# Delta rule and gMLP block: prologue between uv's weight chunks, factors and masks in PSUM, gMLP later in the solve, two of four out_e chunks behind the scan's last step

## The chip, the cores and the metric

The kernel runs on one core of one Trainium2 chip. The metric is the device time of one launch in microseconds. The kernel before has a median of 1855.72 us over 3 runs (1851.77, 1855.72 and 1855.77); its profiled execution took 1853.88 us, of which the profile's span covers 1852.1 us.

## The reference, cut to what matters

The program is a whole two-part network for 256 tokens of width 1024: one block with attention and a large expert layer, then two layers of which the first ("even") has a gMLP half and a gated delta rule half. Only this even layer is touched:

```python
proj = hn @ w_in_e[i]
a_uv, b_qkv, b_z, b_beta, b_a = jnp.split(proj, split_at, axis=-1)
a_out = gmlp_spatial_gate(jax.nn.gelu(a_uv), gmlp_v_gain[i], gmlp_ws[i], gmlp_bs[i])
b_out = gated_deltanet(b_qkv, b_z, b_beta, b_a, gdn_conv[i], gdn_a_log[i],
                       gdn_dt_bias[i], gdn_out_gain[i])
h = h + jnp.concatenate([a_out, b_out], axis=-1) @ w_out_e[i]
...
# gmlp_spatial_gate: v is layer-normed in groups, mixed over the tokens of a chunk, gates u
s = jnp.einsum('gts,bnsgc->bntgc', w, v) + b_s.T[None, None, :, :, None]
return u * s.reshape(bsz, seq, A_WIDTH_2)
...
# chunk_gated_delta_rule: 4 heads, 4 chunks of 64 tokens
decay = jnp.where(causal, jnp.exp(jnp.where(causal, diff, 0.0)), 0.0)
a = jnp.where(strict, jnp.einsum('bhnid,bhnjd->bhnij', k_beta, k) * decay, 0.0)
t_mat = a + jnp.eye(c, dtype=f32)
u = solve(t_mat, v_beta)
w = solve(t_mat, k_beta * jnp.exp(gc)[..., None])
qk = jnp.einsum('bhnid,bhnjd->bhnij', q, k) * decay
def step(state, inp):
    v_new = u_c - jnp.einsum('bhck,bhkv->bhcv', w_c, state)
    o_c = (jnp.einsum('bhck,bhkv->bhcv', q_c, state)
           + jnp.einsum('bhij,bhjv->bhiv', qk_c, v_new))
    state = state * gl_c[..., None, None] + jnp.einsum('bhck,bhcv->bhkv', k_c, v_new)
    return state, o_c
```

## The kernel before, in words

All weights stream through a ring of four slots, one "chunk" of 128 rows by up to 1024 columns at a time, in the order of one list (`PLAN`; `FIRST[name]` is where a matrix begins). The SP queue loads a chunk, ACT rounds it to a high part (`w_hi`, L1208), POOL takes the rest (`w_lo`, L1680), and TensorE (PE) multiplies. A chunk with its weights as moving operand is twelve matmuls of 512 columns (L606 to L608). ACT may round into a slot only when PE has used its last content (`used`), and every engine works through its instructions strictly in the written order, so a wait in front of one instruction holds up all behind it on that engine.

The even layer has, in PE's order, these stages: `qkv_e` with a short convolution on VectorE (DVE); `uv`, 8 chunks for the gMLP half, with six fills of transposes that bring q, k and v to token-major form (`token_major`, tiles `Qt`, `Kt`, `Vt`) ahead of chunk 2; then the delta rule's prologue; the solve; the scan; and `out_e`'s 8 chunks.

- The prologue: `gcT` (cumulated log decay, L975), a diagonal `DG` on DVE (L2322), the decay rows `gcrow` (L981), their differences (`D0`, `decA`, `decAT`, L2327 to L2330) and exponents (ACT, L1503, L1505); key lengths `l2_r` (squares on ACT, L1475, a power on POOL, L1825), three scalings on DVE (`k_map`, `q_map`, `kb_map`, L2309), `QDt` and `KBE` on ACT (L1514), and eight groups of transposes (L996) whose results DVE and ACT copy in turn (`fT`). Masks are multiplied in on DVE (L2344). ACT also applies gelu to uv's four banks (`ev_uv`, L1482, L1486) and squares them for the layer norm (L1497); POOL normalizes them (L1759 to L1771, semaphore `gv`).
- The solve is the list `SOLVE` of 21 products, `a`, `aT`, `N2` and so on to `qkT` (L1046), each for two halves of the tokens: eight matmuls, in six PSUM banks in turn. Where a result is in `PLAIN`, ACT evacuates it, else DVE. At `MIX_AT` the gMLP mix (L1026) stands ahead of the product, DVE makes its result (`OC`, L2358) ahead of the next one's, and at `GMLP_T_AT` stand the transposes of that result.
- The scan has four steps (`wS` L1063, `dS` L1073, `o_T` L1077). After the scan, `head_norm` (ACT squares L1544, POOL power L1844, DVE L2407) gives the other half of `OC`, which is transposed (L679) and streamed into `out_e`'s chunks 4 to 7. Chunks 0 to 3 need only the gMLP half:

```python
for c in range(SEQ // G_CH):
    ...
    m.then_inc(sem("o_T"), 1)
    out_chunk(c)
```

## Time and profile before

| what | value |
|---|---|
| median of 3 runs | 1855.72 us |
| profiled execution, its span | 1853.88 us, 1852.1 us |
| PE, DVE, ACT, POOL busy, share of the span | 95%, 51%, 50%, 57% |
| chain that ended last, by engine | PE 86%, DVE 6%, ACT 3%, POOL 2%, issue 2% |
| uv chunks 2 to 7 | 1119.0 to 1135.6 us |
| prologue, PE busy | 1135.6 to 1155.4 us, 10.6 us |
| solve | 1155.4 to 1206.6 us |
| scan with out_e chunks 0 to 3 | 1206.6 to 1233.1 us |
| wait, transposes, out_e chunks 4 to 7 | 1233.1 to 1255.2 us |

Times count from the span's start. The chain is followed backwards from the last instruction, so an engine's share of it says how much of the span hangs on that engine; busy shares alone do not.

### The profile page before, as it was taken

To read this page: it belongs to the slowest core of one execution; us is meant where nothing else is said; L and a number is where in the kernel's file an instruction comes from. 1 tells how busy PE (TensorE), PEld (TensorE's weight loads), DVE (VectorE), ACT (ScalarE), POOL (GpSimd) and SP (SyncE) were. 2 spreads that over 40 slices of the span, in tenths; PEclk is the share of its full clock that TensorE was granted. 3 is DMA by queue.
4 is the path that set the end of the run, shared out by engine and by line. 5 is a ranking of instruction groups with operands and counts; after the bars stand their busy time and mean duration, and the time that the engine had idled before them with its cause. 6 is when DMAs were issued, how large, how long until landed. Compare 5 with 4: busy or idle time off the path is not lost.

```text
span 1852.1 us, 32185 instructions
## 1 busy us (share of the span) xinstructions
...
## 2 busy tenths in 40 slices
...
GB/s 200 175 80 114 117 213 168 184 182 182 147 139 137 143 143 180 193 193 194 193 193 193 172 191 78 8 84 154 184 190 187 164 159 125 36 163 182 190 185 111
DMA packets 81027, 288.23 MB, mean 156 GB/s; under 512 B 9264, under 2 KB 9264, under 8 KB 80432
## 3 DMA queue, kind: packets, MB, share of 16 engines
...
q10 hardware_dynamic: 432, 1.05, 0.1%
...
## 4 chain that ended last, share of the span: by engine, by line
PE 86%; DVE 6%; ACT 3%; POOL 2%; issue 2%; DMA 0%; DVEq 0%; ACTq 0%; POOLq 0%
PE acc L606 14%; PE acc L607 14%; PE acc L608 14%; PE col L642 11%; PE col L643 11%; PE col L644 11%; PE mb L899 3%; POOL w_lo L1680 1%; PE acc L1046 1%; PE col L1046 1%; ACT hT_hi L1232 1%; PE mb L679 1%; ACT w_hi L1208 1%; PE mb L738 1%; PE mb L880 0%
## 5 line engine op out<-in xcount | busy, mean ns | idle before, releaser
L1680 POOL TENSOR_TENSOR w_lo<-w_raw,w_hi 128x1024 fp32r<-128x1024 f32 (+1 forms) x410 | 989.6, 2434 | 372.8 <-ACT w_hi L1208 372.6
L1208 ACT ACTIVATE w_hi<-w_raw 128x1024 fp32r<-128x1024 f32 (+1 forms) x539 | 565.6, 1053 | 407.1 <-PE acc L608 368.0
L642 PE MATMUL col<-hT_hi,w_hi 128*128 128x256 f32 x1632 | 467.7, 287 | 2.3 <-DVE hT_lo L1886 1.8
L644 PE MATMUL col<-hT_hi,w_lo 128*128 128x256 f32 x1632 | 461.6, 283 | 0.0
L643 PE MATMUL col<-hT_lo,w_hi 128*128 128x256 f32 x1632 | 461.5, 283 | 0.0
L642 PEld LDWEIGHTS col<-hT_hi,w_hi 128*128 128x128 f32 x1632 | 312.5, 192 | 5.4 <-issue 2.2
L643 PEld LDWEIGHTS col<-hT_lo,w_hi 128*128 128x128 f32 x1632 | 312.7, 192 | 2.4
L644 PEld LDWEIGHTS col<-hT_hi,w_lo 128*128 128x128 f32 x1632 | 312.3, 191 | 0.0
L606 PE MATMUL acc<-w_hi,W_hi 128*128 128x512 f32 x512 | 199.2, 389 | 0.0
L607 PE MATMUL acc<-w_lo,W_hi 128*128 128x512 f32 x512 | 199.2, 389 | 0.0
L608 PE MATMUL acc<-w_hi,W_lo 128*128 128x512 f32 x512 | 199.2, 389 | 0.0
L606 PE MATMUL acc<-w_hi,hT_hi 128*128 128x512 f32 (+2 forms) x432 | 171.0, 396 | 15.5 <-POOL w_lo L1680 6.0
L1722 POOL TENSOR_SCALAR_AFFINE_SELECT WST<-WST 128x512 f32<-128x512 f32 x1 | 1.7, 1712 | 318.8 <-DMA WST<-in_gmlp_w 318.8
L2453 DVE CAST H_hi<-H_q 128x256 fp32r<-128x256 f32 x64 | 29.9, 467 | 292.4 <-ACT H_q L1561 292.4
L607 PE MATMUL acc<-w_lo,hT_hi 128*128 128x512 f32 (+2 forms) x432 | 168.4, 390 | 0.0
L608 PE MATMUL acc<-w_hi,hT_lo 128*128 128x512 f32 (+2 forms) x432 | 167.6, 389 | 0.0
L2229 DVE TENSOR_TENSOR w_lo<-w_raw,w_hi 128x1024 fp32r<-128x1024 f32 x128 | 156.4, 1222 | 2.1 <-ACT w_hi L1208 1.9
L2207 DVE TENSOR_TENSOR W_lo<-act_e,W_hi 128x256 fp32r<-128x256 f32 x128 | 54.5, 426 | 145.8 <-ACT W_hi L1417 145.2
L606 PEld LDWEIGHTS acc<-w_hi,hT_hi 128*128 128x128 f32 x432 | 83.2, 193 | 37.0 <-issue 14.9
L606 PEld LDWEIGHTS acc<-w_hi,W_hi 128*128 128x128 f32 x512 | 96.1, 188 | 20.1
L607 PEld LDWEIGHTS acc<-w_lo,W_hi 128*128 128x128 f32 x512 | 96.1, 188 | 19.9
L608 PEld LDWEIGHTS acc<-w_hi,W_lo 128*128 128x128 f32 x512 | 96.1, 188 | 19.8
...
## 6 DMA issues: line engine op xcount, KB each, us to landing
w_raw<-in_expert_u SPq DMA_DIRECT2D x128, 512.0 KB, 3.4
w_raw<-in_expert_v SPq DMA_DIRECT2D x128, 512.0 KB, 3.4
w_raw<-in_w_mlp SPq DMA_DIRECT2D x128, 512.0 KB, 3.4
...
```

The costliest lines, as they stand in the source:

```text
L606: mm(o, hi(t), w_hi[:, s, a:b], start=first, stop=False)
L607: mm(o, hi(t), w_lo[:, s, a:b], start=False, stop=False)
L608: m = mm(o, lo(t), w_hi[:, s, a:b], start=False, stop=last)
L642: mm(o, wh[:, k, :], hi[:, k, :], start=k == 0, stop=False)
L643: mm(o, wh[:, k, :], lo[:, k, :], start=False, stop=False)
L644: m = mm(o, wl[:, k, :], hi[:, k, :], start=False, stop=k == KD - 1)
L899: m = mm(mb[s % 2][:, t * P:(t + 1) * P], hot2[:, s % 2, t, :], hot1[:, s % 2, t, :], start=True, stop=True)
L1046: m = mm((acc + col)[n % 6][:, h * P:(h + 1) * P], maps[lhsT][:, t, h, :], maps[rhs][:, t, h, :], start=True, stop=True)
L1208: f(w_hi[:, s, 0:w], w_raw[:, s, 0:w], ACT.Copy).then_inc(sem(f"hi{s}"), 1)
L1680: g.tensor_tensor(w_lo[:, s, 0:w], w_raw[:, s, 0:w], w_hi[:, s, 0:w].bitcast(F32), ALU.subtract).then_inc(sem(f"lo{s}"), 1)
L2207: v.tensor_tensor(lo[:, q, :], act_e[:, c, :], hi[:, q, :].bitcast(F32), ALU.subtract).then_inc(sem("W_lo"), 1)
L2229: v.tensor_tensor(w_lo[:, s, :], w_raw[:, s, :], w_hi[:, s, :].bitcast(F32), ALU.subtract).then_inc(sem(f"lo{s}"), 1)
```

## The change

What it does, engine by engine:

- PE: `gcT` stands between the fourth and fifth fill of `token_major`, in the banks `col`; the decay rows stand ahead of uv's chunk 3 (`decay_rows`), the two halves of the feature maps ahead of chunks 6 and 7 (`feature_maps(0)`, `(1)`). The solve starts after chunk 7 without waiting for all of uv's banks; its bank order is changed, and its second to fifth half products wait for uv's evacuations one by one. The mix goes from the fifth product to the twelfth, the gMLP transposes from the eleventh to the sixteenth. In the scan, chunk 0 stands behind step 0, none behind step 1, chunk 1 behind step 2, chunks 2 and 3 behind step 3.
- DVE: the decay work comes ahead of the scalings. Masks 0, 1 and 3 and the three factors are copied into PSUM (`map_mask`, `map_scale`), and five multiplications read them there; so does `DG`. A tile `decN` (mask 3 times `decATm`) is new, and `N1T` is made from the PSUM product and `decN`.
- ACT: exponents, `QDt`, `KBE` and the odd `fT` copies come ahead of uv's gelus, with the first three `out_e` chunks' `w_hi` between; the layer norm's squares go behind `N2T`, and write to `N8`. The chunks' `w_hi` behind the scan's steps are placed one by one.
- POOL: the key lengths and `VBt` go ahead of uv's chunk 6, the gain on `Z` ahead of `out_e`'s chunk 0, the rest of the delta and gMLP maps ahead of its chunk 3, with `KDt` first. The second half's output norm stands ahead of chunk 6.

```diff
-MIX_AT, GMLP_T_AT = 4, 10
+MIX_AT, GMLP_T_AT = 11, 15
...
+        solve_banks = [col[1]] + acc + [col[0]]
+        map_scale = [col[0][:, 8 * i:8 * i + 8] for i in range(3)]
+        map_mask = [col[0][:, P * (i + 1):P * (i + 2)] for i in range(3)]
...
+                maps = [[(h * P, QKVF[:, 4 * m + h, t * P:(t + 1) * P]) for h in range(G_H)]
+                        for m in range(3) for t in range(NT)]
+                fills("tok", maps[0:4])
+                for t in range(NT):
+                    mm(col[t][:, 0:G_H], masks[:, 2, :], stat[:, 16 + 4 * t:20 + 4 * t], start=True,
+                       stop=True).then_inc(sem("gcT"), 1)
+                fills("tok", maps[4:6], n0=4)
+            def decay_rows():
+                pe.wait_ge(sem("ones"), 1)
+                for t in range(NT):
+                    pe.wait_ge(sem("diag"), t + 1)
+                    mm(col[t][:, :], ones[:, :], DG[:, t, :, :].rearrange("p h f -> p (h f)"),
+                       start=True, stop=True).then_inc(sem("gcrow"), 1)
+            def feature_maps(t):
...
+            row_group("uv", None, before=(2, token_major, 3, decay_rows, 6, lambda: feature_maps(0),
+                                          7, lambda: feature_maps(1)))
...
+                    if 1 <= n <= 4:
+                        pe.wait_ge(sem("ev_uv"), upto("ev_uv", n))
...
-                out_chunk(c)
+                for k in ((0,), (), (1,), (2, 3))[c]:
+                    out_chunk(k)
...
+            split_to(FIRST["uv"] + 7)
+            act.wait_ge(sem("gc"), 2)
+            f(egc[:, :], gc[:, :], ACT.Exp).then_inc(sem("egc"), 1)
+            for t in range(NT):
+                act.wait_ge(sem("gdiff"), 2 * t + 1)
+                f(decA[:, t, :, :], decA[:, t, :, :], ACT.Exp, scale=-1.0).then_inc(sem("dec"), 1)
+                act.wait_ge(sem("gdiff"), 2 * t + 2)
+                f(decAT[:, t, :, :], decAT[:, t, :, :], ACT.Exp).then_inc(sem("dec"), 1)
+                act.wait_ge(sem("glast"), t + 1)
+                f(gl[:, 8 * t:8 * t + 8], gl[:, 8 * t:8 * t + 8], ACT.Exp).then_inc(sem("gl"), 1)
             split_to(FIRST["uv"] + 8)
+            act.wait_ge(sem("egc"), upto("egc", 1))
+            def times_egc(dst, src, ready, name):
+                act.wait_ge(sem(ready), upto(ready, 1))
+                for t in range(NT):
+                    for h in range(G_H):
+                        x = f(dst[:, t, h, :], src[:, t, h, :], ACT.Copy,
+                              scale=egc[:, 4 * t + h:4 * t + h + 1])
+                x.then_inc(sem(name), 1)
+            def odd_maps(ns):
+                for n in ns:
+                    act.wait_ge(sem("fT_T"), upto("fT_T", n + 1))
+                    f(fT[:, n % 4, n // 4, :, :].rearrange("p h d -> p (h d)"), mb[1][:, :],
+                      ACT.Copy).then_inc(sem("fT_A"), 1)
+            times_egc(QDt, Qt, "q_map", "qd")
+            split_to(FIRST["out_e"] + 1)
+            odd_maps((1, 3))
+            times_egc(KBE, KBt, "kb_map", "kbe")
+            odd_maps((5, 7))
+            split_to(FIRST["out_e"] + 3)
...
+                if s == 4:
+                    gate_squares()
+                if result == "N8":
+                    act.wait_ge(sem("v_ss"), upto("v_ss", 1))
...
-                split_to(FIRST["out_e"] + (6 if t == 0 else KD))
+                split_to(FIRST["out_e"] + 5 + t)
...
+            split_to(FIRST["out_e"] + 7)
             stream_hi("oc", range(2, 4))
+            split_to(FIRST["out_e"] + KD)
...
+                if j == FIRST["uv"] + 6:
+                    key_lengths()
+                    beta_values()
...
-                if j == FIRST["out_e"]:
+                    gate_gain()
+                if j == FIRST["out_e"] + 3:
                     delta_and_gmlp_maps()
...
-                if j in (FIRST["out_e"] + 6, FIRST["mlp0"]):
-                    t = int(j == FIRST["mlp0"])
+                if j in (FIRST["out_e"] + 5, FIRST["out_e"] + 6):
...
+                then(v.tensor_copy(gc[:, 4 * t:4 * t + 4], col[t][:, 0:4]), "gc")
                 then(v.tensor_tensor(DG[:, t, :, :], over(ident[:, :], [P, 4, P], 1),
-                                     over(gc[:, 4 * t:4 * t + 4], [P, 4, P], 2), ALU.mult), "diag")
+                                     over(col[t][:, 0:4], [P, 4, P], 2), ALU.mult), "diag")
+            for n in (4, 5):
+                dve.wait_ge(sem("tok_T"), upto("tok_T", n + 1))
+                then(v.tensor_copy(token[n], mb[n % 2][:, :]), "tok_E")
             for t in range(NT):
...
+            for i, m in enumerate((0, 1, 3)):
+                go(v.tensor_copy(map_mask[i], masks[:, m, :]))
+            go(v.tensor_copy(map_scale[2], stat[:, 32:40]))
...
+            go(v.tensor_copy(map_scale[0], sq16[:, 8:16]))
+            then(v.tensor_scalar(map_scale[1], sq16[:, 0:8], G_DK ** -0.5, None, ALU.mult))
+            scale_groups(Kt, Kt, map_scale[0], "k_map")
+            scale_groups(Qt, Qt, map_scale[1], "q_map")
+            scale_groups(KBt, Kt, map_scale[2], "kb_map")
...
+            for n, (dst, src, m) in enumerate(((decA, decA, 0), (decATm, decAT, 1),
+                                               (decN, decATm, 2))):
+                then(v.tensor_tensor(groups(dst), groups(src), over(map_mask[m], [P, 8, P], 1),
                                      ALU.mult))
+                if n == 0:
+                    even_maps((4, 6))
...
-                        then(v.tensor_tensor(four(aT, t), src, four(decATm, t), ALU.mult))
-                        then(v.tensor_tensor(four(N1T, t), four(aT, t),
-                                             over(masks[:, 3, :], [P, 4, P], 1), ALU.mult), "sv_E")
+                        go(v.tensor_tensor(four(aT, t), src, four(decATm, t), ALU.mult))
+                        then(v.tensor_tensor(four(N1T, t), src, four(decN, t), ALU.mult), "sv_E")
```

The prediction speaks of three places. The first is PE around uv's last chunk. Before, the last matmuls of chunk 7 (`L606` to `L608` lines) are followed by the whole prologue and the solve (`L1046`):

```order
L607 MATMUL acc<-w_lo,hT_hi 128x512
L608 MATMUL acc<-w_hi,hT_lo 128x512
L975 MATMUL mb<-stat,masks 128x4 x2
L981 MATMUL acc<-DG,ones 128x512 x2
L996 MATMUL mb<-ident,Kt 128x128 x4
L996 MATMUL mb<-ident,KBt 128x128 x4
L996 MATMUL mb<-ident,Qt 128x128 x4
L996 MATMUL mb<-ident,QDt 128x128 x4
```

After the change, chunk 6's last matmuls (lines L611 to L613 now) are followed by the second half of the feature maps, and chunk 7 begins behind them:

```order
L612 MATMUL acc<-w_lo,hT_hi 128x512
L613 MATMUL acc<-w_hi,hT_lo 128x512
L997 MATMUL mb<-ident,Kt 128x128 x4
L997 MATMUL mb<-ident,KBt 128x128 x4
L997 MATMUL mb<-ident,Qt 128x128 x4
L997 MATMUL mb<-ident,QDt 128x128 x4
L611 MATMUL acc<-w_hi,hT_hi 128x512
L612 MATMUL acc<-w_lo,hT_hi 128x512
```

What moved is the prologue's PE work, from behind chunk 7 to in front of chunks 3, 6 and 7; the copies of `fT` that its groups wait for now hold up uv's chunks.

The second place is ACT between the squares of k and the solve. Before, uv's gelus (`UV`) and their table come first:

```order
L1482 ACT_TABLE_LOAD
L1482 ACTIVATE UV<-acc,sum_91 128x512
L1486 ACTIVATE UV,gsum<-acc,sum_91 128x128 x4
L1482 ACTIVATE UV<-acc,sum_91 128x512
L1486 ACTIVATE UV,gsum<-acc,sum_91 128x128 x4
L1492 ACT_TABLE_LOAD
L1492 ACTIVATE egc<-gc 128x8
L1497 ACTIVATE N2T,gvar<-UV,gsum 128x128 x8
L1503 ACTIVATE decA<-decA 128x512
```

After the change the gelus come last, behind the copies of `fT` and two chunks' `w_hi`:

```order
L1506 ACTIVATE QDt<-Qt,egc 128x128 x8
L1218 ACTIVATE w_hi<-w_raw 128x1024
L1514 ACTIVATE fT<-mb 128x512 x2
L1506 ACTIVATE KBE<-KBt,egc 128x128 x8
L1514 ACTIVATE fT<-mb 128x512 x2
L1218 ACTIVATE w_hi<-w_raw 128x1024 x2
L1526 ACT_TABLE_LOAD
L1526 ACTIVATE UV<-acc,sum_91 128x512
L1530 ACTIVATE UV,gsum<-acc,sum_91 128x128 x4
L1526 ACTIVATE UV<-acc,sum_91 128x512
L1530 ACTIVATE UV,gsum<-acc,sum_91 128x128 x4
L1560 ACTIVATE N_164<-acc 128x512
```

What moved: a whole group of ACT work is now between PE's feature maps and the evacuation of uv's banks, and the squares (`L1497` before) are no longer in it.

The third place is DVE around the twelfth and thirteenth product of the solve (`Y+` and `YT+`). Before, the additions to `YI` and `YIT` and the masked `L1T`, `L2T` follow each other; the gMLP result `OC` stood eight products earlier:

```order
L2393 TENSOR_TENSOR L1T<-aT,masks 128x512
L2397 TENSOR_TENSOR YI<-col,YI 128x512
L2393 TENSOR_TENSOR L2T<-aT,masks 128x512
L2397 TENSOR_TENSOR YIT<-acc,YIT 128x512
L2393 TENSOR_TENSOR L2T<-aT,masks 128x512
L2397 TENSOR_TENSOR YIT<-acc,YIT 128x512
```

After the change `OC` stands between them:

```order
L2443 TENSOR_TENSOR L1T<-aT,masks 128x512
L2447 TENSOR_TENSOR YI<-col,YI 128x512
L2409 SCALAR_TENSOR_TENSOR OC<-mb,cols,UV 128x128 x8
L2443 TENSOR_TENSOR L2T<-aT,masks 128x512
L2447 TENSOR_TENSOR YIT<-col,YIT 128x512
L2443 TENSOR_TENSOR L2T<-aT,masks 128x512
L2447 TENSOR_TENSOR YIT<-acc,YIT 128x512
```

What moved is eight instructions on DVE, into the one run of DVE work that PE waits for late in the solve.

## Rows read from the trace of the kernel before

**Rows 1.** The page, the chain that ended last by engine.

```profile
PE 86%; DVE 6%; ACT 3%; POOL 2%; issue 2%; DMA 0%; DVEq 0%; ACTq 0%; POOLq 0%
```

**Rows 2.** Windows: length, busy of PE, PEld, DVE, ACT, POOL, PE clock, DMA.

```profile
1119.00:1135.60 16.60, 16.54 (x74) 13.36 (x72) 3.86 (x6) 9.66 (x42) 10.64 (x6) 1.00 0.45 148
1135.60:1155.40 19.80, 10.60 (x41) 6.94 (x41) 10.81 (x20) 13.85 (x48) 10.27 (x14) 0.74 0.01 1
1155.40:1168.00 12.60, 7.54 (x49) 7.35 (x50) 12.33 (x10) 2.75 (x9) 8.23 (x3) 0.73 0.00 0
1168.00:1205.50 37.50, 35.64 (x313) 35.00 (x311) 19.57 (x35) 14.69 (x23) 6.31 (x3) 1.00 0.07 17
...
1242.00:1255.20 13.20, 13.08 (x48) 10.56 (x49) 2.58 (x5) 4.40 (x7) 6.11 (x3) 0.83 0.16 44
```

**Rows 3.** Timeline of DVE: start, length, instruction, idle before and its releaser.

```profile
1132.59 0.17 DVE L2314 TENSOR_SCALAR sq<-sq 128x8 f32<-128x8 f32 x1 [12.60 <-POOL sq L1825]
...
1138.46 2.01 DVE L2322 TENSOR_TENSOR DG<-ident,gc 128x512 f32<-128x512 f32 x1
...
1145.27 0.43 DVE L2329 TENSOR_SCALAR decA<-D 128x512 f32<-128x512 f32 x1
...
1156.33 2.80 DVE L2344 TENSOR_TENSOR decATm<-decAT,masks 128x1024 f32<-128x1024 f32 x1
...
1174.27 2.16 DVE L2358 SCALAR_TENSOR_TENSOR OC<-mb,cols,UV 128x128 f32<-128x128 f32 x8
```

**Rows 4.** Groups, 1113 to 1168 us: busy us, mean ns, idle before.

```profile
L1680 POOL TENSOR_TENSOR w_lo<-w_raw,w_hi 128x1024 fp32r<-128x1024 f32 x5 | 11.8, 2388 | 4.6 <-ACT w_hi L1208 4.6
...
L1208 ACT ACTIVATE w_hi<-w_raw 128x1024 fp32r<-128x1024 f32 x5 | 5.0, 1050 | 0.5 <-PE acc L608 0.5
...
L2387 DVE TENSOR_TENSOR N1T<-aT,masks 128x512 f32<-128x512 f32 x2 | 3.5, 1768 | 0.1
...
L1497 ACT ACTIVATE N2T<-UV,gsum 128x128 f32<-128x128 f32 x8 | 3.1, 387 | 0.0
...
L1825 POOL TENSOR_TENSOR sq<-sq,minus_half 128x16 f32<-128x16 f32 x1 | 2.9, 2927 | 0.1
...
L1514 ACT ACTIVATE QDt<-Qt,egc 128x128 f32<-128x128 f32 x8 | 2.4, 386 | 0.0
...
L2309 DVE TENSOR_TENSOR KBt<-Kt,stat 128x1024 f32<-128x1024 f32 x1 | 1.2, 1224 | 0.0
```

**Rows 5.** Timeline of POOL in the prologue, with idle before and its releaser.

```profile
1144.44 1.75 POOL L1761 TENSOR_TENSOR gvar<-gvar,minus_half 128x8 f32<-128x8 f32 x1
...
1149.85 2.35 POOL L1771 TENSOR_TENSOR UV<-UV,rows 128x1024 f32<-128x1024 f32 x1
1155.12 2.94 POOL L1776 TENSOR_TENSOR KDt<-Kt,kdf 128x1024 f32<-128x1024 f32 x1 [2.91 <-DVE kdf L2341]
```

**Rows 6.** Timeline of ACT: first gelu of uv, table load behind the last.

```profile
1133.54 0.69 ACT L1482 ACTIVATE UV<-acc,sum 128x512 f32<-128x512 f32 x1 [6.42 <-PE acc L608]
...
1137.72 1.28 ACT L1492 ACT_TABLE_LOAD   x1
```

**Rows 7.** Timeline of PE in the solve and at the scan's start.

```profile
1164.24 3.78 PE L1046 MATMUL col<-N,N1T 128*128 128x128 f32 x16 [5.06 <-DVE N1T L2387]
...
1169.70 1.95 PE L1026 MATMUL mb<-UV,WST 128*128 128x128 f32 x16
...
1191.91 2.05 PE L1046 MATMUL col<-P,YIT 128*128 128x128 f32 x16 [1.40 <-DVE YIT L2397]
...
1206.61 1.13 PE L1073 MATMUL mb<-Vn,KDt 64*128 64x128 f32 x8 [1.42 <-DVE Vn L2424]
```

**Rows 8.** Windows of the scan: chunk 0, step 2, end of chunk 3 to chunk 4.

```profile
1208.68:1213.20 4.52, 4.52 (x13) 3.32 (x12) 0.68 (x1) 0.00 (x0) 0.00 (x0) 0.62 0.49 169
...
1220.20:1224.20 4.00, 4.00 (x33) 3.53 (x32) 1.42 (x4) 2.22 (x9) 2.58 (x2) 1.00 0.02 4
...
1233.10:1242.10 9.00, 2.06 (x9) 1.57 (x8) 1.83 (x5) 3.39 (x11) 3.61 (x3) 0.68 0.25 83
```

More of the change, by code:

```diff
@@ L1470, in _ @@
             act.wait_ge(sem("tok_E"), upto("tok_E", 4))
-            for m, (src, squares) in enumerate(((Qt, D0), (Kt, N2))):
+            for m, src in enumerate((Qt, Kt)):
                 for t in range(NT):
@@ L1500, in _ @@
-            x.then_inc(sem("v_ss"), 1)
-            for t in range(NT):
-                act.wait_ge(sem("gdiff"), 2 * t + 1)
-                f(decA[:, t, :, :], decA[:, t, :, :], ACT.Exp, scale=-1.0).then_inc(sem("dec"), 1)
-                act.wait_ge(sem("gdiff"), 2 * t + 2)
-                f(decAT[:, t, :, :], decAT[:, t, :, :], ACT.Exp).then_inc(sem("dec"), 1)
-                act.wait_ge(sem("glast"), t + 1)
-                f(gl[:, 8 * t:8 * t + 8], gl[:, 8 * t:8 * t + 8], ACT.Exp).then_inc(sem("gl"), 1)
@@ L1523, in _, with gate_squares @@
-            times_egc(KBE, KBt, "kb_map", "kbe")
+            def gate_squares():
+                act.wait_ge(sem("v_mean"), upto("v_mean", 1))
+                for t in range(NT):
+                    for g in range(M_G):
+                        x = f(N8[:, t, g, :], UV[:, t, 512 + g * P:512 + (g + 1) * P], ACT.Square,
+                              bias=gsum[:, 4 * t + g:4 * t + g + 1],
+                              accum_out=gvar[:, 4 * t + g:4 * t + g + 1])
+                x.then_inc(sem("v_ss"), 1)
+                split_to(FIRST["out_e"] + 4)
@@ L1773, in delta_and_gmlp_maps @@
                                 ALU.mult).then_inc(sem("gv"), 1)
-                pool.wait_ge(sem("kd_factor"), upto("kd_factor", 1))
-                g.tensor_tensor(heads(KDt), heads(Kt), per_head(kdf[:, :]), ALU.mult).then_inc(
-                    sem("kd"), 1)
                 pool.wait_ge(sem("dec"), 4)
@@ L2299, in _ @@
                                  over(stat[:, 60:64], [P, NT, 4], 1), ALU.mult), "g_ready")
-            copies("tok", [m[:, t, :, :].rearrange("p h d -> p (h d)") for m in (Qt, Kt, Vt)
-                           for t in range(NT)])
+            token = [m[:, t, :, :].rearrange("p h d -> p (h d)") for m in (Qt, Kt, Vt)
+                     for t in range(NT)]
+            copies("tok", token[0:4])
             dve.wait_ge(sem("masks"), 20)
```

122 lines of the change are left out of this document (44 added, 78 removed).

## The prediction, made before the changed kernel was run

> **What bounds the kernel now.** I read the page's chain of waits first: 86% of the span hangs on TensorE (PE) [rows 1]. So the change is worth what it takes out of PE's order, and the stages around it are read window by window [rows 2]. In uv's six last chunks PE is full (16.54 of 16.60 us, clock 1.00), while VectorE (DVE) works 3.86 us. Then comes the prologue, 19.80 us with PE busy 10.60 at a mean granted clock of 0.74. In the next 12.60 us it is busy 7.54 at 0.73. From 1168.0 the solve keeps it full (35.64 of 37.50 us). The timeline tells what PE waits for: 5.06 us for N1T before the third product at 1164.24, then 3.78 us for that product at half clock, and 1.40 us for YIT at 1191.91 [rows 7]. In the scan one window stands out: 9.00 us from chunk 3's end to chunk 4, PE busy 2.06 [rows 8].
>
> The groups say why DVE is slow: N1T takes 1768 ns in the mean [rows 4], but one of its two took 0.69; DG took 2.01 and decATm 2.80 [rows 3], for work that takes 0.69 and 1.22 elsewhere (KBt, same shape: 1224 ns [rows 4]). Each slow one ran while POOL worked on SBUF: decATm from 1156.33 to 1159.13, KDt on POOL to 1158.06 [rows 3, 5]; the rest, 1.07 us, is about its own length.
>
> **The change, part by part**, in times of the trace before.
>
> 1. *uv ends later.* Before, chunk 7 ends at 1135.4. Now the prologue's PE work stands before it: 10.60 us at 0.74 is 7.8 us at most at full clock [rows 2]; half of the decay rows' and transposes' time was at the low clock, which gives about 6.1. To it come the waits that PE now has in uv, for the copies of fT. The scalings wait for the key lengths, which came at 1132.5 [rows 3] and lose two w_lo of 2.39 in front of them: 1127.7 or sooner. DVE comes from the decay rows (chunk 2 ends at 1119.1 + 2.8 = 1121.9, the first row takes 0.9): two rounds of 0.7, twice 0.43 and 0.17 (3.6 us with their gaps), then mask and factor copies, some 1.5 by their columns: 1128.1. Three maps of 1.22 [rows 4] end at 1131.9, when chunk 5 ends. QDt on ACT (2.4 us) waits for the second map and ends at 1133.0; a w_hi of 1.05 stands behind it [rows 4], and a copy of fT of some 0.6. So PE waits 0.8 + 0.3 us for ACT and 0.3 us at the third group for DVE. 6.1 + 1.4 = 7.5: uv ends at 1142.9. (Bounds: 6.1, no wait; 7.8 + 1.4 + 2.4 for a w_lo on POOL in front of DVE's small copies of kdf, 11.6.)
> 2. *uv's evacuation.* ACT makes the last fT copy, two w_hi (2.1) and a table load (1.28 [rows 6]) and reaches the first gelu at 1144.2. From first gelu to last took 1133.54 to 1137.7, 4.15 us, half of it for two banks [rows 6]. So banks are free at 1144.9, 1146.3, 1146.9 and 1148.4. The product aT waits for the second, takes 0.9 per half (35.64 us in 313 matmuls of 16 per product, 1.8 [rows 2]), then DVE makes aT and N1T from PSUM, 0.7 each: the third product starts at 1148.7 instead of 1164.24 [rows 7]. **Gain 15.5.**
> 3. *Third and fourth product*, to the next stage: before 1164.24 to 1169.70, 5.46, with 3.78 for the first [rows 7]. Now PE's idle pieces are under 1.2 us each, so I take the full clock: 1.8 + 1.8, 0.4 of waiting for the second N1T and 0.35 for YI, YIT (DVE, two of 1.22, the first behind KDt on POOL). 4.35. **Gain 1.1** (bounds 0 and 1.8).
> 4. *Rest of the solve.* Before 1169.70 to 1206.61, 36.9 us, mix and transposes in it [rows 7]; both are moved, not removed. DVE now makes OC (2.16 [rows 3]) between the additions of the twelfth and thirteenth product, where PE already waited 1.40 for YIT [rows 7]. That is +2.2, and +0.6 because L1T then meets the w_lo of out_e's chunk 3 on POOL; four w_hi in front of u's evacuation are gone, which saves 0.6 at the end. **Loss 2.2** (bounds 0.5 and 5). The scan begins at 1192.0.
> 5. *The mix* is hidden if gv is there. ACT's squares (3.1 and their reads) run 1153.3 to 1156.5; POOL's chain behind them took 1144.1 to 1152.2, 8.1 us [rows 5], so gv comes at 1164.6. PE reaches the mix after seven products from 1153.05, at 1165.6. Cost nothing, by 1 us; without this cover each us late is a us lost.
> 6. *Scan.* 1206.61 to 1255.2 was 48.6. Step 1 has no chunk behind it: 2.9 less, but the step's DVE work goes on after PE's end (1.42 us of 2.9 fall into the 4.00 window [rows 8]), so 1.4 idle: gain 1.5. Chunks 2 and 3 stand behind step 3. From its end to chunk 4 it was 3.0 + 9.00 = 12.0, with chunk 7's w_hi and w_lo (1.05 + 2.39 [rows 4]) ahead of the output norm. Without them 8.55, less 0.9 as the transposes stay warm. But the head norm has two SBUF inputs, and POOL's w_lo of chunk 6 falls due in its middle: +1.5. So 9.15, of which 5.5 are two chunks instead of one: gain 2.85. Chunks 4 to 7 took 13.2 at clock 0.83 [rows 2], four warm ones take 11.0: gain 2.2. **Gain 6.6** (bounds 2.5 and 9).
>
> Sum: 15.5 + 1.1 - 2.2 + 6.6 = 21.0. The profiled execution took 1853.88 with a span of 1852.1; the median of the runs shown is 1.84 above it, the lowest 2.1 below. 1853.88 - 21.0 = 1832.9; I say **1833 us**.
>
> **A rule weighed.** DVE's decA (0.43 for 512 columns, twice as fast as reads from PSUM) ran at 1145.27, inside POOL's power of 1144.44 to 1146.19, and lost nothing [rows 3, 5]. The Trainium skill, "SBUF — State Buffer", section "Who interferes with whom", says that a tensor_scalar in such a double rate mode and any GpSimd instruction hold the shared ports for their whole length, the other one blocked. The row differs for a power; for plain arithmetic (DG, decATm) rule and rows agree.
>
> **Rivals.**
> - *POOL holds DVE after all.* If the power of 2.93 us blocks decA, DVE's chain, the maps and all of uv's tail come 2.8 us later: gain 18.2, 1836. If reading a factor from PSUM does not free DVE, it can wait for all that POOL does from 1126 to 1138, two w_lo, one more for out_e, VBt and Z, about 11 us: gain 10, 1844. For it: N1T and decATm. Against the second: aT and D0, which read PSUM, never grew. By the rule of the Trainium skill above the first would happen. Chance 12%.
> - *The clock falls between the scan's steps.* Chunk 0 ran at 0.62 (4.52 us instead of 2.9) after only 1.4 us of idle and 2 us of half-height matmuls [rows 8, 7]. Steps 1 and 2 now stand together, 9.5 us without a dense chunk. If step 2 and chunk 1 run at half clock, +3 to +4: 1837. Chance 12%.
> - *gv is late.* POOL's chain runs into DVE or ACT's squares slip by over 1 us; PE waits at the mix, with DVE's additions behind it. +1 to +3: 1835. Chance 5%.
> - *Better:* no port conflict in the head norm, no wait in uv, and L1T free: +1.5, +1.4, +0.6: 1829 or below. Chance 4%.
> - *Slower than before:* PE's clock falls in uv's tail, where it now waits (1.4 us in pieces), and stays at 1.2 GHz through the solve. Products cost 1.8 more each; all of 1. and 3. and the 17 products left would cost over 35 us, 14 more than the gain. It decides from 12 products at half clock. Before, with 5 us idle, one product was enough to bring it back [rows 7]. Chance 2%.
> - *Nothing comes of it:* uv's chunks wait for maps as long as the prologue took. That needs 16 us more DVE and ACT delay than worked out. Chance 3%.
>
> **How the numbers follow.** Forecast, 1829 to 1838: 62%. The cases up to 1841 and down to 1828 take in most of the first rivals; outside lie PSUM factors that don't help, no gain, slower, and half of the better case, under 2 in 10. The range is 1828 to 1841. A measurement of this kernel tells about 0.3%, 5.6 us, from no change. All but the last two rivals lie below 1850: faster 0.95, same 0.03, slower 0.02.
>
> **What would show it.** uv's chunk 7 ending near 1143 and ACT's first gelu some 1.3 us behind; the third product's start near 1149 at full clock; a wait of 3.5 to 4 us for YIT late in the solve, up from 1.40; no wait before the mix; DG and decATm at 0.69 and 1.22; chunks 4 to 7 at full clock. I am wrong if DVE's decay work stands behind POOL's w_lo, if PE shows long waits before chunks 6 and 7, or if the window clock in steps 1 and 2 is under 0.8.

## The result

The changed kernel took 1841.86 us in the median of nine runs (1831.45 to 1844.17); the kernel before, run beside it, 1852.64 us (1848.46 to 1861.13, nine runs). The ratio is 0.993 (95% interval 0.9916 to 0.9944). A second set gave 1838.83 against 1853.04, ratio 0.9915 (0.990 to 0.993). So the change gains 11 to 14 us where I had said 21. The sign was right, the size was not: 1841.86 lies just above my range's upper end of 1841, 1838.83 inside it.

Nine runs spread over 12.7 us, more than most of the steps in question. The traces show most of the reason: in the fourteen profiled executions of this study the token-major transposes, with which the changed stage begins, start anywhere from 1111.38 to 1117.30 us, though nothing ahead of them was changed. From the stage's end to the span's end it is 596.8 us after and 596.9 before; over all fourteen it is 596.7 to 597.0 in seven and 599.5 to 599.9 in the other seven. So steps of 1 to 3 us are read inside one stretch, from the token-major transposes to the raw transposes of the next stage (those of `X`; "the stage" below), and the medians only tell the larger ones.

Four windows of the stage, cut at the token-major transposes, the first product, the third product (N2), the scan's first dS, and the raw transposes; the columns are those of [rows 2]. First the kernel before:

```profile
1114.81:1155.37 40.56, 30.61 (x136) 22.83 (x137) 17.84 (x29) 25.59 (x92) 25.07 (x21) 0.87 0.23 72
1155.37:1164.24 8.87, 3.81 (x33) 3.62 (x33) 8.66 (x7) 2.19 (x8) 8.27 (x3) 0.83 0.00 0
1164.24:1206.61 42.37, 39.40 (x329) 38.80 (x329) 24.19 (x39) 15.29 (x24) 7.42 (x4) 0.96 0.08 24
1206.61:1255.23 48.62, 41.65 (x209) 33.36 (x210) 13.80 (x29) 12.06 (x28) 20.12 (x12) 0.86 0.25 79
```

and the changed kernel:

```profile
1113.40:1142.45 29.05, 26.02 (x137) 20.62 (x138) 23.36 (x36) 22.07 (x68) 22.45 (x11) 1.00 0.36 119
1142.45:1148.54 6.09, 4.26 (x34) 3.72 (x32) 3.06 (x6) 5.30 (x19) 4.45 (x4) 1.00 0.45 142
1148.54:1195.54 47.00, 40.95 (x328) 39.99 (x329) 24.99 (x39) 15.85 (x37) 13.74 (x14) 0.93 0.05 16
1195.54:1239.48 43.94, 40.08 (x208) 32.44 (x209) 15.88 (x29) 12.06 (x28) 18.14 (x11) 0.92 0.20 62
```

The stage takes 126.08 us instead of 140.42: 14.3 less. (The two profiled executions, 1853.88 and 1837.99 us, lie 15.9 apart; 1.4 of that is the earlier start of the changed one's stage, which is not the change's.) The first two windows give 11.51 + 2.78 = 14.3 and the scan 4.7; the third, the solve from N2 on, gives 4.6 **back**. It is the only window whose clock got worse (0.96 to 0.93). PE's order is seen in its timeline, the places that answer to [rows 7] and [rows 8]:

```profile
1138.76 0.66 PE L997 MATMUL mb<-ident,Qt 128*128 128x128 f32 x4 [1.77 <-DVE fT L2382]
...
1148.54 1.13 PE L1055 MATMUL acc<-N,N1T 128*128 128x128 f32 x8 [0.65 <-DVE N1T L2438]
...
1171.86 1.16 PE L1055 MATMUL acc<-YI,L1T 128*128 128x128 f32 x8 [0.29 <-DVE YI L2447]
1176.95 2.07 PE L1055 MATMUL acc<-P,YIT 128*128 128x128 f32 x8 [3.94 <-DVE YIT L2447]
1178.82 1.91 PE L1055 MATMUL col<-P,YIT 128*128 128x128 f32 x8
1180.53 1.92 PE L684 MATMUL mb<-ident,OC 128*128 128x128 f32 x8
```

The first line is the one long wait in uv, for a copy of fT. Eight matmuls take 1.13 us at the third product and 2.07 behind the wait of 3.94. Windows over the wait, the stretch behind it, the scan's chunk 0, its empty step 1, and chunks 4 to 7 (these two groups answer to [rows 8] and the last of [rows 2]):

```profile
1171.86:1176.95 5.09, 1.16 (x8) 0.96 (x8) 4.90 (x12) 0.94 (x2) 0.00 (x0) 0.92 0.04 13
1176.95:1182.20 5.25, 5.25 (x24) 5.25 (x25) 1.38 (x2) 0.58 (x1) 0.00 (x0) 0.50 0.00 0
...
1198.50:1203.70 5.20, 5.20 (x13) 3.79 (x12) 0.68 (x1) 0.00 (x0) 0.00 (x0) 0.52 0.00 0
1203.70:1209.29 5.59, 4.13 (x33) 3.55 (x33) 2.77 (x6) 1.17 (x2) 2.36 (x1) 1.00 0.12 30
...
1228.46:1239.48 11.02, 11.02 (x48) 9.07 (x49) 2.39 (x4) 4.89 (x7) 8.52 (x4) 1.00 0.37 112
```

Two stretches run at the lower of the two clocks (0.50 and 0.52 of 2.4 GHz): the 5.25 us behind the wait for YIT, and chunk 0 (with the eight matmuls `o_T` in front of it, 1.89 us instead of 1.02). DVE's timeline shows two more places, in uv and ahead of the wait:

```profile
1122.22 0.43 DVE L2356 TENSOR_SCALAR decA<-D 128x512 f32<-128x512 f32 x1
...
1133.30 3.42 DVE L2389 COPY kdf<-decAT 64x8 f32<-64x8 f32 x2
...
1168.01 1.62 DVE L2443 TENSOR_TENSOR L1T<-aT,masks 128x512 f32<-128x512 f32 x1 [3.77 <-PE acc L1055]
...
1171.84 2.16 DVE L2409 SCALAR_TENSOR_TENSOR OC<-mb,cols,UV 128x128 f32<-128x128 f32 x8
1174.03 0.69 DVE L2443 TENSOR_TENSOR L2T<-aT,masks 128x512 f32<-128x512 f32 x1
1174.76 0.69 DVE L2447 TENSOR_TENSOR YIT<-col,YIT 128x512 f32<-128x512 f32 x1
1175.48 0.69 DVE L2443 TENSOR_TENSOR L2T<-aT,masks 128x512 f32<-128x512 f32 x1
1176.21 0.69 DVE L2447 TENSOR_TENSOR YIT<-acc,YIT 128x512 f32<-128x512 f32 x1
```

The second YIT, for which PE waits, has OC and two L2T in front of it. And two copies of eight columns took 3.42 us; POOL's timeline tells what they ran beside:

```profile
1122.34 3.10 POOL L1776 TENSOR_TENSOR sq<-sq,minus_half 128x16 f32<-128x16 f32 x1
...
1131.97 2.37 POOL L1791 TENSOR_TENSOR Z<-Z,rows 128x1024 f32<-128x1024 f32 x1
1134.30 2.40 POOL L1705 TENSOR_TENSOR w_lo<-w_raw,w_hi 128x1024 fp32r<-128x1024 f32 x1
```

The two copies end at 1136.72, w_lo at 1136.70.

### The profile page after: what moved, and what is told of

The parts are those of the page before. It is cut to its first block, busy times and chain, and to the rows that moved or that the text cites. A ratio compares the mean times of both kernels' runs of the same rounds, so it can differ in the third digit from the quotient of the medians.

```text
span 1836.3 us, 32192 instructions
## 1 busy us (share of the span) xinstructions
PE 1746.2 (95%) x10852; PEld 1563.1 (85%) x10852; DVE 941.9 (51%) x1874; ACT 922.2 (50%) x1592; POOL 1051.6 (57%) x542
## 4 chain that ended last, share of the span: by engine, by line
PE 86%; DVE 6%; ACT 4%; POOL 2%; issue 2%; DMA 0%; DVEq 0%; ACTq 0%; POOLq 0%
PE acc L611 14%; PE acc L612 14%; PE acc L613 14%; PE col L647 11%; PE col L648 11%; PE col L649 11%; PE mb L904 3%; POOL w_lo L1705 2%; PE acc L1055 1%; ACT hT_hi L1242 1%; PE mb L684 1%; ACT w_hi L1218 1%; PE col L1055 1%; PE mb L743 0%; PE mb L885 0%
## 5 line engine op out<-in xcount | busy, mean ns | idle before, releaser
L611 PE MATMUL acc<-w_hi,W_hi 128*128 128x512 f32 x512 | 199.2, 389 | 0.0
L613 PE MATMUL acc<-w_hi,W_lo 128*128 128x512 f32 x512 | 199.2, 389 | 0.0
L611 PE MATMUL acc<-w_hi,hT_hi 128*128 128x512 f32 (+2 forms) x432 | 170.6, 395 | 16.1 <-POOL w_lo L1705 6.0
L613 PE MATMUL acc<-w_hi,hT_lo 128*128 128x512 f32 (+2 forms) x432 | 167.1, 388 | 0.0
L611 PEld LDWEIGHTS acc<-w_hi,hT_hi 128*128 128x128 f32 x432 | 82.7, 191 | 37.5 <-issue 15.3
L613 PEld LDWEIGHTS acc<-w_hi,W_lo 128*128 128x128 f32 x512 | 96.1, 188 | 20.1
L611 PEld LDWEIGHTS acc<-w_hi,W_hi 128*128 128x128 f32 x512 | 96.1, 188 | 20.0
```

The source lines that it names most:

```text
L611: mm(o, hi(t), w_hi[:, s, a:b], start=first, stop=False)
L613: m = mm(o, lo(t), w_hi[:, s, a:b], start=False, stop=last)
```

## The experiments

Each run's segments, in us, are differences between the starts of the same four instructions in PE's timeline: the token-major transposes, the third product N2, the scan's first dS, and the raw transposes. Each ratio is to the kernel before run on the same chip beside it (its medians: 1852.64 for the first run of the change; 1853.04 for the next four; 1853.34 for the masks, kdf and the two parts alone; 1854.25 for the last four).

| kernel | to N2 | N2 to scan | scan, out_e | stage | median, us | ratio to before, 95% |
|---|---|---|---|---|---|---|
| before | 49.43 | 42.37 | 48.62 | 140.42 | 1852.64 | |
| changed | 35.14 | 47.00 | 43.94 | 126.08 | 1841.86 | 0.993, 0.9916 to 0.9944 |
| changed, second set | 35.13 | 47.11 | 43.91 | 126.15 | 1838.83 | 0.9915, 0.990 to 0.993 |
| OC one step later | 35.13 | 42.32 | 45.55 | 123.00 | 1838.18 | 0.9917, 0.9896 to 0.9938 |
| PE kept busy | 35.15 | 44.16 | 43.70 | 123.01 | 1839.11 | 0.9927, 0.9911 to 0.9943 |
| one chunk behind each step | 35.15 | 47.08 | 47.51 | 129.74 | 1838.75 | 0.9918, 0.9904 to 0.9931 |
| masks in SBUF | 41.06 | 45.57 | 43.72 | 130.35 | 1843.19 | 0.9945, 0.9927 to 0.9962 |
| kdf on ACT | 33.75 | 45.94 | 43.76 | 123.45 | 1841.39 | 0.9928, 0.9908 to 0.9949 |
| before, scan's part alone | 49.48 | 42.04 | 45.43 | 136.95 | 1850.82 | 0.9989, 0.9979 to 1.0000 |
| before, mix later alone | 49.32 | 46.74 | 46.99 | 143.05 | 1857.56 | 1.0019, 1.0006 to 1.0033 |
| OC during P2 | 35.14 | 41.45 | 43.63 | 120.22 | 1834.43 | 0.9892, 0.9869 to 0.9915 |
| and L1T, L2T early | 35.15 | 38.85 | 42.39 | 116.39 | 1832.19 | 0.9877, 0.9856 to 0.9898 |
| and kdf on ACT | 33.74 | 38.85 | 43.86 | 116.45 | 1832.88 | 0.9883, 0.9862 to 0.9904 |
| and work in the scan's waits | 33.76 | 39.62 | 42.62 | 116.00 | 1830.18 | 0.9880, 0.9859 to 0.9901 |

The trace of one execution agrees with the next to 0.1 us where the clock doesn't differ ("to N2": 35.13 to 35.15 in the seven executions where that part is the changed kernel's). The changed kernel again was run under

> The changed kernel itself, as the yardstick of this set. Theory: the ratio to before is 0.993 again, and the trace shows the same four places as its first trace: a copy of kdf of 3.4 us on VectorE behind POOL's w_lo, a wait of about 3.9 us for YIT late in the solve with TensorE at half clock in the 5.2 us behind it, and the scan's chunk 0 at half clock (5.2 us). Rival: these places came from one disturbed execution; then the half-clock stretches lie elsewhere or are gone, and the wait for YIT stays under 3 us.

The wait was 3.94 us again, the stretch behind it 5.23 us at 0.50, chunk 0 5.30 us at 0.52. These are the kernel's own, not one execution's.

**OC one step later.** What is late at the thirteenth product?

```
-                if s == MIX_AT + 1:
+                if s == MIX_AT + 2:
```

> The changed kernel with OC (the gate's product, 2.16 us on VectorE) made one step later, behind the additions of the thirteenth product instead of in front of them. Theory (my step 4, the wait for YIT is OC standing in front): the wait of 3.9 us shrinks to about 1.7, the clock does not fall behind it (5.2 us become 2.6), but TensorE waits 0.4 to 0.8 us for OC before the transposes, and P2's product gets its subtraction about 1 us later: 2 to 4 us faster than the changed kernel, ratio to before 0.991 to 0.992. Rival A (the wait comes from L1T and POOL's w_lo on the port): the wait stays at 3 us or more and nothing is gained. Rival B (the clock falls with or without the long wait): the wait shrinks by 2.2, the half-clock stretch stays, gain about 2.

PE's timeline and the window behind the wait:

```profile
1175.72 1.16 PE L1055 MATMUL acc<-P,YIT 128*128 128x128 f32 x8 [1.75 <-DVE YIT L2447]
```

```profile
1175.72:1180.97 5.25, 5.11 (x44) 4.92 (x45) 4.27 (x12) 1.08 (x2) 0.00 (x0) 1.00 0.00 0
...
1203.99:1209.56 5.57, 5.57 (x32) 4.95 (x32) 1.44 (x4) 1.16 (x8) 1.26 (x2) 0.69 0.18 72
```

The wait is 2.19 shorter, OC's length, and the same 5.25 us now hold 44 matmuls instead of 24. Rivals A and B fall; N2 to the scan is 4.7 us shorter. But the scan now gives 1.6 back: step 0 is 1.6 shorter than in the changed kernel (chunk 0 took 4.54 us at 0.62), the third step (0.69) is 1.6 longer and chunks 4 to 7, 12.62 us at 0.86, are 1.6 longer. The median does not tell the 3.1 us of the trace from nothing.

**PE kept busy.** Is it the idle time that takes the clock down? Only PE gets work here, 14 matmuls that nobody reads, and DVE stays as it was:

```
+                if s == 14:
+                    pe.wait_ge(sem("sv_E"), solved(NT * s - 5)[0])
+                    pe.wait_ge(sem("sv_A"), solved(NT * s - 5)[1])
+                    for i in range(14):
+                        mm(solve_banks[NT * s % 6][:, 0:P], maps["N1"][:, 0, i % G_H, :],
+                           maps["N1"][:, 0, i % G_H, :], start=True, stop=True)
```

> The changed kernel with 14 extra 128-column matmuls of N1 with itself (3.2 us at full clock) in front of TensorE's wait for YIT, into the bank that the fifteenth product overwrites next: results that nobody reads. The wait itself is not made shorter. Theory (the 3.9 us without work take the clock down): the wait shrinks to under 1 us, the 5.25 us behind it run at full clock, 2.6 us faster than the changed kernel. Rival (the clock falls for another reason, as the half-full products or the first us of the mix): the 5.25 us stay at half clock and the time is that of the changed kernel; if the fillers themselves run long, slower by up to 1 us.

```profile
1171.67:1176.77 5.10, 4.29 (x37) 4.09 (x37) 4.91 (x12) 0.93 (x2) 0.00 (x0) 1.00 0.04 16
1176.77:1182.02 5.25, 5.25 (x47) 5.25 (x48) 2.50 (x4) 1.08 (x2) 0.00 (x0) 1.00 0.00 0
...
1203.08:1208.61 5.53, 5.53 (x33) 5.05 (x33) 1.45 (x4) 1.16 (x8) 1.26 (x2) 0.71 0.17 67
1223.75:1236.19 12.44, 12.44 (x49) 10.13 (x50) 2.39 (x4) 4.89 (x7) 8.50 (x4) 0.88 0.34 100
```

YIT comes 5.10 us after the second half of P1 starts, as in the changed kernel (5.09), but the stretch behind it is at full clock: N2 to the scan 2.84 us shorter, with DVE's work unchanged. So a wait of 3.94 us for YIT costs 3.94 and then another 2.6 to 2.8 for the clock. This is the part of the loss that the prediction did not have. The wait itself fell from 3.94 to 0.81 us only because 3.13 us of fillers stand in it. The last two lines are the scan's third step and chunks 4 to 7: chunk 0 now ran at 1.00, but these two lost the clock, which they had kept in the changed kernel, and the scan took 43.70 us against 43.94. The median (ratio 0.9927) shows nothing of the 3.1 us of the stage.

**One chunk behind each step.**

```
-                for k in ((0,), (), (1,), (2, 3))[c]:
+                for k in ((0,), (1,), (2,), (3,))[c]:
```

> The changed kernel with one chunk of out_e behind each step of the scan, as before the change, while everything else of the change stays (the split of the weights and the output norm's roots keep their new places). Theory (my step 6: an empty step 1 gives back 1.5 us and two chunks behind the last step hide the output norm, 2.85 us): the scan to the raw transposes takes 3 to 4 us longer than in the changed kernel, ratio to before 0.9945 to 0.9955. Rival (chunks 2 and 3 are worth no more behind step 3, since the steps between them lose the clock): within 1 us of the changed kernel, or faster, if the chunk behind step 1 keeps the clock up in step 2 and chunk 1.

The scan took 47.51 us instead of 43.94, 3.6 longer, inside what the theory said. The wait for OC (the output norm) is back, 3.91 us instead of 1.35, and chunks 4 to 7 took 12.89 us at 0.84 instead of 11.02. The median shows nothing of it (ratio 0.9918, expected 0.9945 to 0.9955): 3.6 us are within what six runs miss here.

**Masks and factors in SBUF.** The five copies to PSUM are left out, and DG, the maps and the masks read `gc`, `sq16`, `stat` and `masks` where they lie:

```
-                                     over(col[t][:, 0:4], [P, 4, P], 2), ALU.mult), "diag")
+                                     over(gc[:, 4 * t:4 * t + 4], [P, 4, P], 2), ALU.mult), "diag")
...
-                then(v.tensor_tensor(groups(dst), groups(src), over(map_mask[m], [P, 8, P], 1),
+                then(v.tensor_tensor(groups(dst), groups(src), over(masks[:, m, :], [P, 8, P], 1),
```

> The changed kernel with the three masks, the key lengths, beta and DG's decays read from SBUF instead of from the PSUM bank that the change copies them to (the copies are left out). The stage from the token-major transposes to the raw transposes takes 126.1 us in the changed kernel and 140.4 before. Theory (PSUM operands are what keeps VectorE free while POOL works): the maps and the masks now stand behind POOL's w_lo, VBt and Z; PE waits for fT in uv's last chunks, uv ends 6 to 11 us later and the stage takes 132 to 137 us; ratio to before 0.996 to 0.999. Rival (only small copies collide, the maps' place between POOL's work decides): the stage stays within 2 us of 126.1. Second rival: without the copies VectorE is 1.5 us earlier, and the stage is shorter than 126.

DVE's timeline, and POOL's of the same stretch:

```profile
1118.05 2.58 DVE L2344 TENSOR_TENSOR DG<-ident,gc 128x512 f32<-128x512 f32 x1
...
1122.84 0.43 DVE L2354 TENSOR_SCALAR decA<-D 128x512 f32<-128x512 f32 x1
...
1124.69 2.11 DVE L2354 TENSOR_SCALAR decA<-D 128x512 f32<-128x512 f32 x1
1126.83 2.51 DVE L2355 TENSOR_SCALAR decAT<-D 128x512 f32<-128x512 f32 x1
...
1129.78 1.23 DVE L2362 TENSOR_TENSOR Kt<-Kt,sq 128x1024 f32<-128x1024 f32 x1
...
1132.30 3.25 DVE L2362 TENSOR_TENSOR KBt<-Kt,stat 128x1024 f32<-128x1024 f32 x1
```

```profile
1121.72 2.93 POOL L1774 TENSOR_TENSOR sq<-sq,minus_half 128x16 f32<-128x16 f32 x1
1124.62 1.90 POOL L1781 TENSOR_TENSOR VBt<-Vt,stat 128x1024 f32<-128x1024 f32 x1
1126.47 2.58 POOL L1703 TENSOR_TENSOR w_lo<-w_raw,w_hi 128x1024 fp32r<-128x1024 f32 x1
```

DG took 2.58 us beside a w_lo (0.69 in the changed kernel), which put the second decA and decAT beside VBt and w_lo: 2.11 and 2.51 us for work of 0.43. uv ends 5.9 us later, at the low end of the first theory; the stage takes 4.3 us more and the ratio rises to 0.9945 (its interval overlaps that of the changed kernel's first set), both less than it said, since 1.4 us come back between N2 and the scan (a shorter stretch at low clock). The copies to PSUM took 0.92 us in the changed kernel (1125.20 to 1126.12), and earn that several times over. The two decA in one timeline also settle the prediction's first rival: DVE's 0.43 inside POOL's power (1121.72 to 1124.65) lost nothing, the same instruction beside POOL's product VBt was held until that ended. The Trainium skill, "SBUF — State Buffer", section "Who interferes with whom", has a tensor_scalar in its double rate mode and any GpSimd instruction shut each other out for their whole length. The trace agrees for the product and differs for the power.

**kdf on ACT.** The two small copies go from VectorE to ScalarE, behind its exponentials (shown is what ScalarE gets):

```
+            act.wait_ge(sem("dec"), 4)
+            for c in range(2):
+                rr = slice(G_CH * c, G_CH * c + G_CH)
+                x = f(kdf[rr, :].rearrange("p (t h) -> p t h", t=NT),
+                      decAT[rr, :, :, G_CH * c + G_CH - 1], ACT.Copy)
+            x.then_inc(sem("kd_factor"), 1)
```

> The changed kernel with the two small copies of kdf (64 partitions by 8 numbers, SBUF to SBUF) made by ScalarE behind its exponentials instead of by VectorE, where they took 3.42 us behind POOL's Z and w_lo. Theory (the shared port holds them): VectorE's masks start 3 us sooner, TensorE's wait of 1.8 us for fT before uv's last chunk is 0.3 or gone, the stage from the token transposes to the raw transposes takes 124.3 to 125 us instead of 126.1, unless the mask's own read of SBUF or ACT's later QDt takes it back. Rival (the wait for fT is something else's, such as VectorE's own length): stage within 0.4 us of 126.1.

```profile
1130.38 0.44 ACT L1502 ACTIVATE kdf<-decAT 64x8 f32<-64x8 f32 x2
```

```profile
1141.17 0.66 PE L997 MATMUL mb<-ident,Qt 128*128 128x128 f32 x4 [0.42 <-DVE fT L2387]
```

0.44 us on ACT for what took 3.42 on DVE; PE's wait for fT fell from 1.77 to 0.42 and N2 came 1.39 us sooner. The stage is 2.6 shorter, but only 1.4 of that is kdf's: the rest is a shorter stretch at low clock behind the wait for YIT (4.40 us at 0.61). The median, ratio 0.9928, shows none of it.

**The parts alone.** The kernel before with the scan's part of the diff (chunks, norm roots and splits of the weights at their new places), and the kernel before with `MIX_AT, GMLP_T_AT = 11, 15`:

> The kernel before with the scan's part of the change alone: chunk 0 behind step 1 of the scan, none behind the second, chunk 1 behind the third, chunks 2 and 3 behind the last, and the output norm's roots and the weights' splits in the places of the change. Theory (my step 6 as measured in the pair, 4.7 us, and as forecast, 6.6): the scan to the raw transposes takes 42 to 44 us instead of 48.6, the rest of the kernel is as before: 4.5 to 6.5 us faster, ratio 0.9965 to 0.9975. Rival (the gain needs the late mix, as w_hi in front of u's evacuation and the clock at the scan's start differ): under 2 us.

> The kernel before with the mix and its transposes moved in the solve alone (mix in front of the twelfth product, transposes in front of the sixteenth). Theory (my step 4: OC then stands in front of the thirteenth product's addition, TensorE waits 2.2 us longer for YIT, and the clock falls behind that wait): the stage takes 142 to 145.5 us instead of 140.4, ratio 1.001 to 1.003. Rival (nothing is lost, as POOL's w_lo doesn't meet L1T here, and a wait of under 2 us costs no clock): within 1 us of before, or faster, if the mix at the fourth product had waited for gv.

The scan's part gave 3.2 us in the scan (48.62 to 45.43) and 2.5 in the median (an interval that reaches 1.0000), less than expected: the third step ran partly at half clock (5.59 us at 0.69 instead of 4.00). Chunks 4 to 7 took 12.56 us at 0.87, where the changed kernel had 11.02. The mix moved alone cost 4.4 us between N2 and the scan and 4.2 in the median, the one slower result that stands clear of 1, as the first theory said. The stage took only 2.6 more, as chunk 0 ran at 1.00 there (2.96 us) and the scan was 1.6 shorter. In its trace:

```profile
1195.06 3.79 PE L1046 MATMUL col<-P,YIT 128*128 128x128 f32 x16 [3.66 <-DVE YIT L2397]
```

```profile
1195.06:1200.32 5.26, 5.26 (x24) 5.26 (x25) 1.38 (x2) 0.59 (x1) 0.00 (x0) 0.50 0.00 0
```

much the same wait (3.66 us instead of 3.94) and the same 5.3 us at half clock, with the prologue behind uv as before. Moving the mix is what brings them.

**A version without the wait.** Four kernels, each with one edit more. OC during P2 and its transposes in front of u:

```
-MIX_AT, GMLP_T_AT = 11, 15
+MIX_AT, GMLP_T_AT = 11, 18
...
-                if s == MIX_AT + 1:
+                if s == 16:
```

> The changed kernel with OC made by VectorE while TensorE does P2 (the seventeenth product), and its transposes in front of u instead of in front of the sixteenth product. Stage from the token transposes to the raw transposes: 126.1 us in the changed kernel, 123.0 with OC one step later. Theory (what stands in front of the thirteenth product's addition makes the wait for YIT; a wait under 2 us costs no clock): the wait is 1.4 to 1.8 us as with OC one step later, the scan starts 4.5 to 5.5 us sooner than in the changed kernel; the scan loses one stretch of half clock somewhere (43.5 to 45.5 us). Stage 120.5 to 123. Rival (the end of the solve is bound by VectorE: OC then delays the last subtraction and u): stage 124 to 126.

then L1T and L2T at `s in (10, 13)`, where DVE has no addition to make, instead of between the additions of the twelfth and thirteenth product:

> As the kernel with OC made during P2, and L1T and L2T (VectorE, four of 0.7 to 1.6 us) made while VectorE has nothing to do (during N8 and P1) instead of between the additions. Theory: what is left of the wait for YIT, 1.75 us, is VectorE's L1T and L2T between the additions; it falls to 0 to 0.5 us, and L1T no longer meets POOL's w_lo in front of P1: stage 118.5 to 121. Rival (L1T now meets POOL's work for gv, so gv and the mix come later): a wait of 1 us or more before the mix, no gain over the kernel without it.

then kdf on ACT as above, and last ten and seven unread matmuls ahead of the scan's first product and its third step:

> As the kernel before in this set, with kdf's two copies on ScalarE too. Theory: uv ends 1.4 us sooner as it did alone, and the rest moves along: stage 117 to 119.6, ratio to before 0.986 to 0.989. Rival: gv depends on POOL's w_lo, not on uv's end, and the mix now waits for it; then the 1.4 us are lost again there.

> As the kernel before in this set, with extra 128-column matmuls, whose results nobody reads, in front of two waits of the scan: ten before its first product (1.6 us without work there) and seven before the third step (1.46 us). Theory (the scan's half-clock stretch follows the half-height matmuls and waits of two steps in a row, so work in the waits keeps the clock): no stretch at half clock between the scan's start and chunk 4, the scan to the raw transposes takes 41 to 42.5 us instead of 43.7 to 45.5. Rival (the clock falls at a place that the fillers don't reach, as behind OC's transposes, or falls later instead): the scan takes 43.5 us or more, and if the fillers run into VectorE's release, up to 1 us more.

The first left a wait of 1.74 us and made the solve 5.55 us shorter than the changed kernel's. The second took that wait away too. Its window from N2 to the scan:

```profile
1149.64:1188.49 38.85, 37.35 (x328) 36.91 (x329) 26.15 (x39) 15.73 (x37) 14.64 (x14) 1.00 0.06 21
```

```profile
1165.37 3.50 DVE L2423 TENSOR_TENSOR L1T<-aT,masks 128x512 f32<-128x512 f32 x2
1169.11 0.69 DVE L2447 TENSOR_TENSOR YI<-acc,YI 128x512 f32<-128x512 f32 x1 [0.24 <-PE acc L1055]
```

The two L1T are held by POOL's decQ (3.50 us for 1.4), and nobody waits for them. The stage was 116.39, better than expected (118.5), the median 1832.19, ratio 0.9877: faster than both kernels, its interval ending at 0.9898, just below the 0.990 where that of the changed kernel's second set begins (on another chip). kdf moved N2 by 1.41 again, but the scan lost 1.5 to the clock, and neither stage nor median shows a gain. With work in the scan's waits, the third step ran at 1.00. Chunks 4 to 7, without and with that work:

```profile
1220.94:1233.44 12.50, 12.50 (x49) 10.12 (x49) 2.39 (x4) 4.89 (x7) 8.50 (x4) 0.87 0.30 101
```

```profile
1216.26:1228.89 12.63, 12.63 (x48) 10.20 (x49) 2.38 (x4) 4.89 (x7) 8.49 (x4) 0.86 0.33 102
```

So they were slow without the fillers too, and the rival that the clock falls later instead is not shown. From the scan's start to chunk 4 nothing ran at half clock, as the theory said, and the scan took 42.62 us instead of 43.86. But the fillers ran longer than the waits that they filled: N2 to the scan grew by 0.77 us (38.85 to 39.62) and the scan up to its third step by 0.24, so that the stage gained only 0.45. Nor is it shown that the fillers kept the third step's clock: the kernel with L1T and L2T early had that step at 1.00 (4.00 us) without them.

## Why the prediction was right, and where it was off

**Step 1, uv ends later: right, 1.0 us short.** Against the stage's start the first product came at 29.05 us, forecast 28.1. The 1.0 is the bound I had named and not taken, DVE's kdf copies behind POOL (kdf on ACT: 1.4 us back). The prices of the maps, of DG (0.69 instead of 2.01 [rows 3]) and decATm (1.22 instead of 2.80) were right. PE's waits were not split as forecast: 0.25 us for ACT instead of 1.1, 2.28 for DVE's copies of fT instead of 0.3, of which 1.77 is the one behind kdf. The mask and factor copies took 0.92, forecast 1.5.

**Step 2, the third product: right.** With 1.41 us for the earlier start it gained 14.3, forecast 15.5. Step 3 gained 1.45, forecast 1.1: its two products took 4.01 us at full clock.

**Step 4, the rest of the solve: the step that failed.** Its loss, put at 2.2 with bounds of 0.5 and 5, measured 6.1: 42.99 us from the next stage (1152.55) to the scan against 36.9, outside its own bounds. The mechanism, OC in front of YT+ and L1T beside a w_lo, was right in place: the wait grew from 1.40 to 3.94, forecast 3.5 to 4. What the sum lacked is the half clock that follows a wait of that length: it took the stretch behind the wait at full clock. I put the half clock into the rivals only for uv's tail and the scan, though the kernel before had its own example in view, 3.78 us for a product behind 5.06 us idle [rows 7]. The clock is 2.6 to 2.8 of the 6.1, shown by keeping PE busy; the longer wait is 2.5 (forecast with L1T's share 2.8), a second wait for YI 0.3, the longer wait at the scan's start 0.2. The 0.6 that I had credited for the w_hi in front of u is not seen, and up to 0.4 is not accounted for. (The scan's start was written as 1192.0; the terms give 1192.2. It enters no sum.)

**Step 5, the mix: right.** gv came at 1164.46, the mix started at 1165.06 without a wait, in no kernel here did it wait.

**Step 6, scan: 4.7 instead of 6.6.** From one step's start to the next: the empty step 1 gave 1.42 (6.99 to 5.57; forecast 1.5), the end of step 3 to chunk 4 2.7 (forecast 2.85, with the head norm at 3.32 us as foreseen), chunks 4 to 7 2.1 (forecast 2.2), and step 0 lost 1.6: the matmuls `o_T` ahead of chunk 0 took 1.89 us instead of 1.02, and chunk 0 ran almost wholly at half clock (5.23 us), where it had been partly so before (4.5 us at 0.62 [rows 8]). The single terms held; what I had left unchanged did not stay.

Sum: 14.3 + 1.45 - 6.1 + 4.7 = 14.3 us, forecast 21.0. The missing 6.7 is 1.2 + 3.9 + 1.9, less 0.3 from step 3, and 4.2 to 4.4 of it is clock (2.6 to 2.8 behind YIT, 1.6 in step 0). From the base of 1853.88 the trace's 14.3 give 1839.6. That one set's median lies just above the range and the other's inside it is the runs' spread, and no merit of the sum, which was off by a third.

**The rivals.** POOL's power held nothing (decA beside it took 0.43 us; that is 1.6 times as fast as 0.69 from PSUM, not the twice that I wrote); a PSUM factor does free DVE (masks in SBUF: 5.9 us). "The clock falls between the scan's steps", given 12%, did not happen in the changed kernel's two traces but is real: of eleven profiled executions with an empty step 1 (in one of them the wait behind it was filled), step 2 (the third) ran partly at half clock in seven, at about 1.6 us each (5.57 for 4.00); of the three with a chunk behind each step, in none. "gv late" did not come. I should have taken one stretch of lost clock in the scan as the likely case.

What stays open is which of the scan's places loses the clock. Behind the same wait of 3.94 us for YIT, chunk 0 was at 0.52 (changed kernel, twice, and with one chunk each) or at 1.00 (kdf on ACT, masks in SBUF). With PE busy ahead of YIT the loss went from step 0 to step 2 and chunks 4 to 7. And chunks 4 to 7, dense as they are, ran at 0.83 to 0.88 in every kernel but the changed one, which had them at 1.00 in both its traces. No kernel had the whole scan at full clock.
